# Sums of squares of x on TensorE in four side-by-side tiles, and h's hi and lo parts from the scaled tile

## What is computed

```python
def rms_norm(x, g):
    xf = x.astype(jnp.float32)
    y = xf * lax.rsqrt(jnp.mean(xf * xf, axis=-1, keepdims=True) + RMS_EPS)
    return (y * g.astype(jnp.float32)).astype(x.dtype)

c_act = jax.nn.silu(c)
mod = (c_act @ w_ada[l] + b_ada[l])[:, None, :]
shift, scale, gate = jnp.split(mod, 3, axis=-1)
h = rms_norm(x, g_norm[l]) * (1 + scale) + shift
proj = h @ w_in[l]
```

## Time and profile before

| | us |
|---|---|
| median of 3 runs | 997.03 |
| lowest of the runs | 996.4 |
| profiled execution, its own time | 995.86 |
| its span | 993.7 |
| TensorE busy in the span | 971.8 |
| DVE busy | 694.6 |
| ScalarE busy | 252.7 |

### The profile page before, as it was taken

The page is one execution under the profiler, slowest core; times in us unless marked ns, Lnnn a source line. Parts: engine busy times, 40 slices in busy tenths (PEclk is TensorE's granted clock), DMA queues, the critical chain, the costliest instruction groups (busy, mean ns, idle before and its releaser), DMA issues.

```text
span 993.7 us, 14662 instructions
## 1 busy us (share of the span) xinstructions
PE 971.8 (98%) x6196; PEld 958.9 (97%) x6196; DVE 694.6 (70%) x687; ACT 252.7 (25%) x264; POOL 1.9 (0%) x12
## 2 busy tenths in 40 slices
PE   4999999999999999999999999999999999999997
PEld 3799999999999999999999999999999998999996
DVE  6878988627898772889864689978788743342346
ACT  5531112221122221111222111122633512122242
POOL 0000000000000000000000000000000000000000
PEclk9999999999999999999999999999999999999998
DMA  9611221231131231222024112213871173125104
GB/s 376 246 43 56 95 81 54 85 122 44 64 111 34 86 117 58 64 86 97 27 75 143 43 66 100 65 54 123 320 283 63 30 310 128 44 87 190 43 1 170
DMA packets 31960, 106.39 MB, mean 107 GB/s; under 512 B 7712, under 2 KB 14112, under 8 KB 28448
## 3 DMA queue, kind: packets, MB, share of 16 engines
q1 hardware_dynamic: 28304, 92.82, 26.8%
q10 hardware_dynamic: 3600, 12.72, 3.3%
HBM read 82.74 MB, written 22.79 MB: 106 GB/s over the span
## 4 chain that ended last, share of the span: by engine, by line
PE 96%; DVE 1%; DMA 1%; ACT 1%; SPq 0%; issue 0%; DVEq 0%
PE ps L463 31%; PE ps L466 31%; PE ps L464 31%; DMA bf<-x_t 1%; PE aux L415 1%; DVE stage_hi L886 1%; PE aux L449 0%; PE aux L421 0%; DVE hf L1159 0%; ACT hf L710 0%; PE aux L635 0%; PE aux L627 0%; ACT w_hi L678 0%; ACT L716 0%; SPq L302 0%; DVE bf L900 0%
## 5 line engine op out<-in xcount | busy, mean ns | idle before, releaser
L464 PE MATMUL ps<-hr,w_hi 128*128 128x344 f32 x1536 | 486.7, 320 | 0.0
L463 PE MATMUL ps<-hr,w_hi 128*128 128x344 f32 x1344 | 426.4, 320 | 0.0
L928 DVE SCALAR_TENSOR_TENSOR conv_y<-conv_u,par,conv_y 128x1024 f32<-128x1024 f32 x240 | 308.0, 1283 | 20.6 <-PE ps L466 14.1
L464 PEld LDWEIGHTS ps<-hr,w_hi 128*128 128x128 f32 x1536 | 288.9, 188 | 0.0
L466 PE MATMUL ps<-hr,w_lo 128*128 128x344 f32 x1344 | 285.0, 320 | 0.0
L463 PEld LDWEIGHTS ps<-hr,w_hi 128*128 128x128 f32 x1344 | 252.7, 188 | 1.7 <-issue 1.7
L466 PEld LDWEIGHTS ps<-hr,w_lo 128*128 128x128 f32 x1344 | 224.7, 188 | 0.0
L678 ACT ACTIVATE w_hi<-w_raw 128x1024 fp32r<-128x1024 f32 (+1 forms) x88 | 87.5, 996 | 270.8 <-PE ps L466 270.8
L862 DVE TENSOR_TENSOR w_lo<-w_raw,w_hi 128x1024 fp32r<-128x1024 f32 (+1 forms) x88 | 101.2, 1150 | 52.0 <-ACT w_hi L678 46.7
L463 PE MATMUL ps<-gr,w_hi 128*128 128x344 f32 x384 | 123.3, 323 | 0.0
L464 PE MATMUL ps<-gr,w_hi 128*128 128x344 f32 x384 | 121.8, 320 | 0.0
(11 more groups left out here) (128 smaller groups left out, 590.8 us busy)
## 6 DMA issues: line engine op xcount, KB each, us to landing
w_raw<-w_main SPq DMA_DIRECT2D x80, 512.0 KB, 3.6
ada_raw<-w_ada SPq DMA_DIRECT2D x8, 1024.0 KB, 16.9
bf<-x_t SPq DMA_DIRECT2D x4, 1032.0 KB, 8.6
sig_a<-stage_lo ACTq DMA_DIRECT2D x8, 516.0 KB, 2.7
sig_b<-stage_hi ACTq DMA_DIRECT2D x8, 516.0 KB, 2.6
y_conv<-conv_y SPq DMA_DIRECT2D x8, 516.0 KB, 2.9
silu_z<-stage_hi ACTq DMA_DIRECT2D x8, 516.0 KB, 4.2
bf<-y_conv SPq DMA_DIRECT2D x4, 1032.0 KB, 6.9
```

Of the source, the lines that this page charges most:

```text
L463: nc.tensor.matmul(out, wh, rhs_hi[:, cols(c)], start=(k == 0), stop=False)
L464: nc.tensor.matmul(out, wh, rhs_lo[:, cols(c)], start=False, stop=False)
L928: return v.scalar_tensor_tensor(out=y, in0=conv_u[:, x, k:k + SEQ], scalar=par[:, x, k:k + 1], in1=y, op0=ALU.mult, op1=ALU.add)
```

## The change

- **Sums.** DVE no longer adds squares. TensorE takes each squared tile as it comes: `square_sums(e)` cuts the 1032 tokens into four parts of 258 (`QCOLS`) and gives each its own 32-column tile of the array, so that part g ends on the partitions 32g to 32g+31, accumulated over the eight tiles in PSUM. Three fillers follow each of the groups 1 to 6.
- **Root and spread.** The root and the reciprocal are taken once on 128x258. `spread_rstd` brings the parts back to all partitions by four products with a one-hot weight (a column of `eye`, broadcast), and ScalarE and DVE copy two each into `row_rstd`. ScalarE takes the root of one column at the start, behind the Silu, so the load of the root's table stands there.
- **Order on TensorE.** All modulation products now come behind the spread. The first step of jobs 0 and 1 follows the product of chunk 1 and stands ahead of the turn of chunk 1.
- **h.** ScalarE writes the hi part with the shift added straight from the scaled tile (one pass in the place of two); DVE makes the lo part as scaled tile + shift - hi. The sample columns have hi and lo instructions of their own. DVE's order in a pair is now modulation, first tile, samples, second tile, lo, lo.
- **Loads and splits.** Raw weights of jobs 0 and 1 are loaded and split in halves: the first halves ahead of the modulation weights, the second halves behind chunk 0. The small tensors are issued by ScalarE. `eye` is 128x128.

The diff, cut to its core:

```diff
-WARM_SUMS = 10
-WARM_ADA = ((0, 4), (0, 8), (0, 0), (0, 0))
-WARM_TURN = (3, 9, 0, 0)
-WARM_FIRST = 4
+WARM_SUMS = 6
+WARM_TILE = 3
+WARM_SPREAD = 8
+WARM_TURN = 4
+WARM_FIRST = 6
...
+            HALF = KT * P // 2
             for s in range(2):
-                sp.dma_start(w_raw[:, s, :], t["w_main"][s]).then_inc(raw_full[s], 16)
+                sp.dma_start(w_raw[:, s, 0:HALF], t["w_main"][s][:, 0:HALF]).then_inc(first_half_loaded[s], 16)
...
+                if q == 0:
+                    for s in range(2):
+                        sp.dma_start(w_raw[:, s, HALF:], t["w_main"][s][:, HALF:]).then_inc(raw_full[s], 16)
...
+            def square_sums(e):
+
+                for g in range(QUADS):
+                    quad = slice(g * QUAD, (g + 1) * QUAD)
+                    last = nc.tensor.matmul(x_sums[quad, :], ones[:, 0:QUAD], hf[:, e, g * QCOLS:(g + 1) * QCOLS],
+                                            start=(e == 0), stop=(e == KT - 1), tile_position=(0, g * QUAD))
+                return last
+
+            def spread_rstd():
+
+                pe.wait_ge(x_inverse_ready, 1)
+                for g in range(QUADS):
+                    nc.tensor.matmul(rstd_bank[g], eye[:, g * QUAD:g * QUAD + 1].broadcast_to([P, P]), x_rstd,
+                                     start=True, stop=True).then_inc(x_spread, 1)
...
-            pe.wait_ge(x_squared, KT - 2)
-            keep_warm(WARM_SUMS)
-            pe.wait_ge(x_summed, 1)
-            token_sums(aux[:, 0, 0:CW], sq_sum[:, cols(0)], x_var_done)
-            token_sums(aux[:, 1, 0:CW], sq_sum[:, cols(1)], x_var_done)
-            token_sums(ps[:, 1, 1, 0:CW], sq_sum[:, cols(2)], x_var_done)
+            for e in range(KT):
+                pe.wait_ge(x_squared, e + 1)
+                if e == 0:
+                    keep_warm(WARM_SUMS)
+                last = square_sums(e)
+                if 0 < e < KT - 1:
+                    keep_warm(WARM_TILE)
+            last.then_inc(x_var_done, 1)
+            keep_warm(WARM_SPREAD)
+            pe.wait_ge(small_loaded, 64)
+            spread_rstd()
...
+            act.wait_ge(ones_ready, 1)
+            nc.scalar.activation(eps[:, 2:3], eps[:, 0:1], ACT.Sqrt)
...
-                nc.scalar.activation(bf[:, e, 0:SEQ], bf[:, e, 0:SEQ], ACT.Identity, bias=mod[:, e // 2, e % 2, 0:1]).then_inc(h_shifted, 1)
-                act.wait_ge(h_shifted, e + 1)
-                nc.scalar.activation(hr[:, e, :], bf[:, e, :], ACT.Copy).then_inc(h_hi_done, 1)
+                nc.scalar.activation(hr[:, e, 0:SEQ], bf[:, e, 0:SEQ], ACT.Identity, bias=mod[:, q, j, 0:1]).then_inc(h_hi_done, 1)
+                if j == 0:
+                    act.wait_ge(h_samples_ready, q + 1)
+                    nc.scalar.activation(hr[:, e:e + 2, SEQ:TOK], bf[:, e:e + 2, SEQ:TOK], ACT.Copy).then_inc(h_samples_hi, 1)
...
-            for e in range(1, KT):
-                dve.wait_ge(x_squared, e + 1)
-                link(v.tensor_tensor(sq_sum, hf[:, 0, :] if e == 1 else sq_sum, hf[:, e, :], ALU.add))
-            dve.sem_inc(x_summed, 1)
...
+            dve.wait_ge(x_std_ready, 1)
+            v.reciprocal(x_rstd, x_rstd).then_inc(x_inverse_ready, 1)
+            first_split(0, 0)
+            first_split(1, 0)
+            for g in range(2, QUADS):
+                dve.wait_ge(x_spread, g + 1)
+                link(v.tensor_copy(row_rstd[:, g * QCOLS:(g + 1) * QCOLS], rstd_bank[g]))
...
-                v.tensor_tensor(hr[:, KT + e, :], bf[:, e, :], hr[:, e, :].bitcast(F32), ALU.subtract).then_inc(h_lo_done, 1)
+                v.scalar_tensor_tensor(out=hr[:, KT + e, 0:SEQ], in0=bf[:, e, 0:SEQ], scalar=mod[:, q, j, 0:1], in1=hr[:, e, 0:SEQ].bitcast(F32),
+                                       op0=ALU.add, op1=ALU.subtract).then_inc(h_lo_done, 1)
```

More of the change, by code:

```diff
@@ L47 @@
 QUADS = P // QUAD
+QCOLS = TOK // QUADS
 TOKBS = 4
@@ L427, in keep_warm, with ada @@
                 for _ in range(n):
-                    nc.tensor.matmul(ps[:, 0, 0, 0:P], ones[:], ones[:], start=True, stop=True)
-            def ada(q, half):
-                if (q, half) == (0, 0):
+                    nc.tensor.matmul(ps[:, 1, 1, 0:P], ones[:], ones[:], start=True, stop=True)
+            def ada(q):
+                if q == 0:
                     pe.wait_ge(c_ready, 1)
-                if q >= 2 and half == 0:
-                    pe.wait_ge(x_std_ready, 4 - q)
-                keep_warm(WARM_ADA[q][half])
-                pe.wait_ge(ada_loaded[q][half], 16)
-                for k in range(half * KT // 2, (half + 1) * KT // 2):
-                    last = modulation_product(ada_bank[q], k, ada_raw[:, q, :, :])
-                if half == 1:
-                    last.then_inc(ada_done, 1)
+                if q == 2:
+                    pe.wait_ge(x_std_ready, 1)
+                if q == 3:
+                    pe.wait_ge(ada_mod_done, 2)
+                for half in range(2):
+                    pe.wait_ge(ada_loaded[q][half], 16)
+                    for k in range(half * KT // 2, (half + 1) * KT // 2):
+                        last = modulation_product(ada_bank[q], k, ada_raw[:, q, :, :])
+                last.then_inc(ada_done, 1)
             def turn(q):
-                keep_warm(WARM_TURN[q])
                 pe.wait_ge(ada_rows_ready, q + 1)
                 modulation_turn(ada_bank[q], ada_rows[:, q % 2, :]).then_inc(ada_turned, 1)
+            def square_sums(e):
[9 more added lines that the diff above has]
+                                     start=True, stop=True).then_inc(x_spread, 1)
             def token_sums(out, row, done):
@@ L494, in _, with first_steps @@
             together = KT - 3
-            def side_by_side(k):
+            def first_steps(k, jobs=(0, 1)):
                 if k == 0:
                     pe.wait_ge(w_lo_done, 2)
-                    pe.wait_ge(ada_mod_done, 2)
-                    pe.wait_ge(x_std_ready, CHUNKS)
+                if k == KT // 2:
+                    pe.wait_ge(w_lo_done, 4)
                 pe.wait_ge(h_lo_done, k + 1)
-                h_step(0, k)
-                h_step(1, k)
-            for q in range(4):
-                ada(q, 0)
-                ada(q, 1)
-                if q == 0:
-                    pe.wait_ge(small_loaded, 64)
-                if q >= 2:
-                    pe.wait_ge(h_lo_done, q)
-                    h_step(0, q - 1)
-                if q == 3:
-                    h_step(1, q - 1)
-                turn(q)
-                if q == 2:
-                    h_step(1, q - 1)
-                if q == 1:
-                    keep_warm(WARM_FIRST)
-                    side_by_side(0)
-            for k in range(3, together):
-                side_by_side(k)
+                for i in jobs:
+                    h_step(i, k)
+            ada(0)
+            keep_warm(WARM_TURN)
+            turn(0)
+            keep_warm(WARM_FIRST)
+            ada(1)
+            first_steps(0)
+            turn(1)
+            first_steps(1)
+            ada(2)
+            first_steps(2, [0])
+            turn(2)
+            first_steps(2, [1])
+            ada(3)
+            first_steps(3, [0])
+            turn(3)
+            first_steps(3, [1])
+            for k in range(4, together):
+                first_steps(k)
             for i in range(2):
@@ L719, in _ @@
                 h_hi(e)
-                if e % 2 == 0 and e // 2 + 1 < 4:
+                if e % 2 == 1 and e // 2 + 1 < 4:
                     ada_out(e // 2 + 1)
+                if e == 1:
+                    first_split(0, 1)
+                    first_split(1, 1)
             STAGED = {4: (0, "sig_a"), 5: (1, "sig_a"), 6: (2, "sig_b"), 7: (3, "sig_b"), 13: (2, "silu_z"), 15: (3, "silu_z")}
```

92 lines of the change are left out of this document (54 added, 38 removed).

## The result

| | before | changed |
|---|---|---|
| median, us | 996.7 (6 runs, with the three shown above) | 1000.21 (6 runs, 999.92 to 1000.54) |
| profiled execution, its own time | 995.86 | 1000.16 |
| its span | 993.7 | 998.3 |
| first product of h | 33.60 | 36.41 |
| first product of job 2 | 62.26 | 66.78 |

One of the three executions of the kernel before that the first table rests on took 3409.45 us, for a reason that no profile shows, and the ratio leaves it out; the five others lie between 995.42 and 997.03. The ratio of changed to before is 1.0041, with a 95% interval from 1.0031 to 1.0052: slower by some 4 us. The forecast was 1000.0.

A forecast was written before the change was run, and what follows sets the result against it. TensorE's unbroken stream was taken as the bound, so only job 2's start counted: first product at 35.5 plus 30.8 gives 66.3, 4.1 later; 995.86 + 4.1 = 1000.0 us, range 995.0 to 1004.0.

The forecast's parts named there:

- TensorE's part of the sums, the term that decides: TensorE's fillers and groups of squares, 9.34 to 22.4 us: 1.40 per square arriving every 1.04, ending 5.8 behind the last.
- Squares: ScalarE's squares of x at the kernel's start: from 8.3 to 16.6 us, 1.04 each, against an end of 15.83 before.
- The table load: Load of the root's table on ScalarE in front of the squares: 1.28 us, plus 0.2 for a one-column root.
- The further 1.4 of the rule: Rival, chance 0.10: a drain at the table load, or small transfers, move squares and TensorE's start by 1.4, total 1001.4.
- From variance to first product: Root, reciprocal, spreads, ada(0), turn, modulation, scaling, hi and lo: first product of h at 35.5 us instead of 33.60.
- From first product to job 2: TensorE's stretch up to job 2: 28.66 us before, 30.8 after, so job 2 starts at 66.3, 4.1 later.
- The extra turn: One turn more on TensorE between first product and job 2, 0.9 us.
- Both waits that I priced at 1.2 together: TensorE waits 0.4 for tile 2's lo part and 0.8 at turn(3), between first product and job 2.
- The other side: Rival, chance 0.12: TensorE keeps up with the squares, variance at 17.2, job 2 at 61.1, total 994.8.
- the clock rival: Rival, chance 0.18: TensorE reaches 2.4 GHz later; 1.1 us more if 6.8 after the start, up to 17 in all.

The follow-up runs named there:

- the last runs: The changed kernel with edits joined: all four, 994.21 us; no fillers between groups and turn of chunk 1 early, 993.2 us, with variants at 994.02, 994.13 and 994.3 us.

## Why the prediction was right

- **TensorE's part of the sums, the term that decides.** Right in kind, and 0.7 too small. Start 9.21 (forecast 9.34). A group and three fillers at the high rate take 1.44 (16.71 to 18.14), forecast 1.40. The size that was off is the rise of the rate: I took 4.4 us behind the first product, this profile shows 6.1 (the three fillers from 13.92 to 15.27 are still slow, 0.5 more than forecast). Root at 23.17, forecast 22.5. The run without the fillers takes 6.5 away and leaves nothing of the lag.
- **Squares.** 8.02 to 15.94, forecast 8.3 to 16.6; a square in a row of eight takes 0.99, not 1.04. It didn't matter, since TensorE is behind.
- **The table load.** 1.28 by its row, and 1.40 from its start to the first square (6.62 to 8.02). Moving it back gave 1.6 at the start of the squares. The further 1.4 of the rule in "ScalarE: Activation LUTs", What ACT_TABLE_LOAD costs, of the Trainium skill, is in none of the profiles: the row of the next activation starts when the load's ends (6.62 + 1.28, next 7.91).
- **From variance to first product.** The reciprocal took 1.77 (1.73), the spreads 1.98, DVE's two copies 0.93, so the last part of `row_rstd` was ready at 28.1 (27.05): 0.7 of this is the root, the rest the spreads and the copies. DVE waited 3.33 for turn(0) (3.5), and the scaling started 1.0 later than forecast, of which 0.7 is the root. First product 36.41, forecast 35.5; TensorE waited 1.82 (1.7). The run with the modulation product in front shows that its place was worth 2.9.
- **From first product to job 2.** 30.37, forecast 30.8. The extra turn is there (0.81 in place of 0.9). Both waits that I priced at 1.2 together came, but smaller. The step of tile 2 starts 2.06 behind the modulation product in front of it (43.14 to 45.20), where the same place took 1.86 in the kernel before, so it waited 0.2 for the lo part; turn(3) waited 0.33 by its row. With the first product 0.9 late and this stretch 0.4 short, two errors partly cancel, and that is luck.
- **The rest.** 4.52 at job 2, forecast 4.1, and nothing but 0.1 behind it. The total also hangs on the number it was added to. I took the profiled execution, 995.86, against a median of 997.03, which stood on three executions with the one of 3409.45 among them. In the later sessions the kernel before has medians of 995.6 to 995.9 over 15 to 27 executions each, so the profile was a common one; from 997.03 the forecast would have been 1001.1, 0.9 too high.
- **The rivals.** The other side (TensorE keeps up) did not happen here, but the run without fillers between groups is that case: root at 16.63, job 2 at 60.26, 2.0 before the kernel before; I had 61.1. The small end of the clock rival came in part: it had the rise at 6.8 behind the first product, and it came at 6.1 and not at 4.4. The profiles of three kernels whose lists are the same up to the root show how much this moves: from first product to root 13.96, 12.98 and 13.31. As the main cause of the loss the clock is out, since without the fillers between the groups the loss is gone, although the rate rises only during the groups there as well.

What became of the gain, then: the reciprocals are 5.2 us shorter (6.98 to 1.77), and h's part gives 0.55 by its profile. Against that stand, each measured by undoing it alone, the fillers with 6.5, the place of the modulation product with 2.9, the turn behind the steps with 1.1, and the early table load with 1.6 (1.6 of start; its profile's other 0.7 is the rate's). They don't add up to 4.5: each was measured with the others in place, and the last runs show how they depend on each other.

The best kernels of the study are the changed one without fillers between the groups (993.47, ratio 0.9978) and the same with the turn moved (993.2, ratio 0.9975); the intervals don't tell them apart, and the first has its ten times within 0.55 us, the second its eleven within 2. Both are faster than both kernels of the case, by 0.2% against the kernel before. Not tried: fillers in the tail right before the last spread (six stand further ahead, at 986.76 in the changed kernel, in front of the final norm's sums), and an earlier load of chunk 1's modulation weights, which is what TensorE waits for once the sums are early.

## What to carry to other kernels

Work that fills an engine's waits must be shorter than the waits: before a filler or a small product is put between two pieces of real work, compare its time per piece with the interval at which the pieces arrive (here 1.44 us of work for each square that comes every 0.99). When a sum is moved to the engine that bounds the kernel, look at what stands behind it in that engine's list and was early until then, because it is now late by as much. And re-measure each gain after the others are in: a reorder and a moved table load that were worth 2.9 and 1.6 us while the sums were late cost time together once they were early. Last, look where else two profiles of the study differ before a difference of 1 us is put down to an edit: here the first landing, the moment of the clock's rise and the last spread of the kernel each moved a profile by 0.4 to 1 us.

## What the runs showed of the hardware

- The rise of TensorE's rate from 1.2 to 2.4 GHz came 6.1 us behind the first product in the changed kernel's profile, against 4.4 before. Rows of the same instructions show it in other kernels, too: the first two groups took 1.95, 1.78 and 1.45 us. From first product to root these three took 13.96, 13.31 and 12.98, so it moves the head by up to 1.0 us.
- The granted clock column reads 1.00 in the first microseconds, where products run at half their later rate. It shows a fall later in the kernel (0.50), but not the low level at the start. Durations of equal products are the safer sign.
- Four 32-column tiles of 258 columns side by side take 0.57 us to the start of the filler behind them, and raise the rate without whole-array products in front: with groups alone the last slow one ended 3.4 us behind the first start (8.93), and the next, at 12.65, was fast.
- A fall of the clock behind short waits (0.78 and 0.72 us in one profile, 0.65 and 0.72 in a second, TensorE busy for 1.2 to 1.4 of each 2 us between 26 and 30) hit two profiled executions and spared a third with waits of 0.86 and 0.72, and a fourth with 0.58 and 1.03.
- The same eight records at the end of the kernel took 1.12, 1.30 or 2.0 us, by where the fall of the clock in that tail came.
